# Second attention stage: logits as three products of high and low parts, and transposes three places behind the logits

## The reference, cut to what matters

```python
def diff_mixer(h, rel_bias, w_in, ..., lambda_init):
    proj = h @ w_in
    q = proj[..., :B_WIDTH].reshape(bsz, L, 2 * B_HEADS, B_HEAD_DIM) * (B_HEAD_DIM ** -0.5)
    k = proj[..., B_WIDTH:2 * B_WIDTH].reshape(bsz, L, 2 * B_HEADS, B_HEAD_DIM)
    v = proj[..., 2 * B_WIDTH:3 * B_WIDTH].reshape(bsz, L, B_HEADS, 2 * B_HEAD_DIM)
    ...
    def block(args):
        logits = jnp.einsum('bqmd,blmd->bmql', qb, k).astype(jnp.float32)
        logits = logits + jnp.moveaxis(bias, -1, 0)[None]
        logits = jnp.where((rel >= 0)[None, None], logits, -jnp.inf)
        p = jax.nn.softmax(logits, axis=-1).reshape(bsz, B_HEADS, 2, BLOCK_Q, L)
        a = p[:, :, 0] - lam * p[:, :, 1]
        return jnp.einsum('bhql,blhe->bqhe', a.astype(v.dtype), v)
```

## Time and profile before

| | us |
|---|---|
| median of 3 runs | 4052.26 |
| lowest and highest | 4047.88, 4061.18 |
| the profiled execution | 4043.49 |
| its span, first to last instruction | 4041.6 |
| TensorE busy | 3491.7 (86% of the span) |
| VectorE busy | 2131.5 (53%) |
| ScalarE busy | 2029.4 (50%) |
| GpSimd busy | 503.2 (12%) |
| mean granted TensorE clock | 0.935 |

### The profile page before, as it was taken

The page is one execution under the profiler, slowest core; times in us unless marked ns, Lnnn a source line. Parts: engine busy times, 40 slices in busy tenths (PEclk is TensorE's granted clock), DMA queues, the critical chain, the costliest instruction groups (busy, mean ns, idle before and its releaser), DMA issues. The chain is left out here.

```text
span 4041.6 us, 63580 instructions
## 1 busy us (share of the span) xinstructions
PE 3491.7 (86%) x18242; PEld 2545.4 (63%) x18242; DVE 2131.5 (53%) x5809; ACT 2029.4 (50%) x3495; POOL 503.2 (12%) x544
## 2 busy tenths in 40 slices
PE   7837798866799999998793999999978888889599
PEld 6725554446566666665683888889945555555487
DVE  2617989998455555554664000000067777777344
ACT  2516778972677777776224111111156666666222
POOL 1000045300111111111120111111000000000011
PEclk9968999986899999999896999999989999999789
DMA  6474277754232222222542222212121111110443
...
DMA packets 400008, 406.94 MB, mean 101 GB/s; under 512 B 73264, under 2 KB 325584, under 8 KB 398288
## 3 DMA queue, kind: packets, MB, share of 16 engines
...
## 5 line engine op out<-in xcount | busy, mean ns | idle before, releaser
L1119 DVE CUSTOM_DVE_ANT_0 a_att_sb_lg<-a_att_ps_s,mask 128x512 f32<-128x512 f32 (+3 forms) x512 | 302.2, 595 | 241.6 <-PE a_att_ps_s L1013 199.4
L393 ACT ACTIVATE b_qkgv_sb_o_lo<-b_qkgv_ps_acc 128x512 f32<-128x512 f32 x128 | 76.6, 599 | 637.5 <-PE b_qkgv_ps_acc L376 472.3
L1150 DVE MEMSET b_att_sb_mx<- 128x256 f32 x1 | 0.3, 272 | 721.6 <-PEq L88 721.6
L1193 ACT ACTIVATE a_att_sb_pT<-a_att_ps_t 128x512 f32<-128x512 f32 (+3 forms) x640 | 316.6, 530 | 106.7 <-PE a_att_ps_t L1029 98.4
L1185 ACT ACTIVATE b_att_sb_lg<-b_att_sb_lg,b_att_sb_negm 128x384 f32<-128x384 f32 (+15 forms) x256 | 305.7, 1198 | 112.5 <-DVE b_att_sb_negm L1127 112.0
L1121 DVE TENSOR_SCALAR_CACHE_REDUCE b_att_sb_lg<-b_att_ps_s 128x512 f32<-128x512 f32 (+3 forms) x512 | 289.8, 591 | 133.7 <-PE b_att_ps_s L1018 125.8
L1185 ACT ACTIVATE a_att_sb_lg<-a_att_sb_lg,a_att_sb_negm 128x384 f32<-128x384 f32 (+15 forms) x256 | 307.3, 1201 | 79.2 <-DVE a_att_sb_negm L1127 79.2
L1012 PE MATMUL a_att_ps_s<-a_att_sb_k,a_att_sb_q 128*128 128x512 f32 (+3 forms) x640 | 287.9, 450 | 67.0 <-DMA a_att_sb_k<-scratch_kT 45.2
L1029 PE MATMUL a_att_ps_t<-ident,a_att_sb_lg 128*128 128x128 f32 x2176 | 340.0, 279 | 0.0
L1018 PE MATMUL b_att_ps_s<-b_att_sb_k,b_att_sb_q 64*128 64x512 f32 (+3 forms) x1280 | 323.6, 592 | 14.5 <-DMA b_att_sb_k<-scratch_kT 9.9
L1540 DVE TENSOR_SCALAR_CACHE_REDUCE mask<-scores,threshold_bits 128x384 bf16<-128x384 f32 (+8 forms) x288 | 322.5, 1186 | 1.2
...
## 6 DMA issues: line engine op xcount, KB each, us to landing
...
a_att_sb_q<-scratch_qT SPq DMA_DIRECT2D x128, 128.0 KB
a_att_sb_q<-scratch_qT SPq DMA_DIRECT2D x256, 64.0 KB
...
```

What stands on the lines that cost most here:

```text
L1119: x = nc.vector.tensor_tensor_reduce(out, src, tab, 1.0, 2 * NEG, ALU.add, ALU.max, top[:, col:col + 1])
L1193: nc.scalar.activation(pT[:, r % 2, a:z, c:c + P], t_ps[:, n % TR, 0:z - a], ACT.Copy).then_inc(t_left, 1)
```

## The change

In `stage_attention` for M = 2, queries and keys come as high and low parts, each of the type F32R: `q` has a part index with two entries and so has `k`. A set of logits is three products for each map: high by high, low by high, high by low (query part first), accumulated in the same bank, map 0 and map 1 by turns. `LAG` is 3 for M = 2 and stays 2 for M = 1; `TAIL` follows from it. Each load of q or k is two transfers. In `b_qkgv` the jobs for q and k are of the kind "split", so both parts are written to memory.

```diff
--- before.py
+++ after.py
@@ -794,7 +794,6 @@
 OR = 2
 QS, OS, KPIECES = 4, 4, 4
 LR, LR2 = 4, 2
-LAG = 2
 PAIR = 2 * P
 
 PAIRS = [1, 3, 5, 7, 6, 4, 2, 0]
@@ -823,6 +822,7 @@
 
 
     V2 = M == 1
+    LAG = 2 if V2 else 3
     width = HD if V2 else P
     SR, TR = (2, 4) if V2 else (4, 2)
     NCHUNK = M * BEFORE[NB]
@@ -838,8 +838,8 @@
     NM = 4
 
     with Stage(nc, sems, name) as st:
-        q = st.sb("q", [P, QS, 2, PAIR], F32R) if V2 else st.sb("q", [P, QS, PAIR], F32)
-        k = st.sb("k", [P, 2, T], F32R if V2 else F32)
+        q = st.sb("q", [P, QS, 2, PAIR], F32R)
+        k = st.sb("k", [P, 2, T] if V2 else [P, 2, 2, T], F32R)
         v = st.sb("v", [P, 2, NB, width], F32)
         v_zero = st.sb("v_zero", [P, HD], F32) if V2 else None
         near, near_next = (st.sb(n, [P, M, NEAR], F32) for n in ("near", "near_next"))
@@ -900,15 +900,18 @@
                     for part in range(2):
                         sp.dma_start(q[(1 - part) * HD:(2 - part) * HD, r % QS, 1].bitcast(F32), q_dram[part, rows, cols]).then_inc(q_in[r % QS], 16)
                 else:
-                    sp.dma_start(q[:, r % QS], q_dram[0, ds(h * P, P), cols]).then_inc(q_in[r % QS], 16)
+                    for part in range(2):
+                        sp.dma_start(q[:, r % QS, part].bitcast(F32), q_dram[part, ds(h * P, P), cols]).then_inc(q_in[r % QS], 16)
 
             def load_k(h, piece):
                 keys = slice(piece * (T // KPIECES), (piece + 1) * (T // KPIECES))
-                dst = k[:, ds(h % 2, 1), keys].rearrange("p o t -> p (o t)")
                 if V2:
+                    dst = k[:, ds(h % 2, 1), keys].rearrange("p o t -> p (o t)")
                     sp.dma_start(dst.bitcast(F32), k_dram[0:2, ds(h * HD, HD), keys]).then_inc(k_in, 16)
                 else:
-                    sp.dma_start(dst, k_dram[0, ds(h * P, P), keys]).then_inc(k_in, 16)
+                    for part in range(2):
+                        dst = k[:, ds(h % 2, 1), part, keys].rearrange("p o t -> p (o t)")
+                        sp.dma_start(dst.bitcast(F32), k_dram[part, ds(h * P, P), keys]).then_inc(k_in, 16)
 
             def load_near(h):
 
@@ -1003,7 +1006,7 @@
                 b, (a, z) = ORDER[p], chunks(ORDER[p])[i]
                 cols = slice((b % 2) * P, (b % 2 + 1) * P)
                 if i == 0 and p % 2 == 0:
-                    loads = 48 if V2 else 16
+                    loads = 48 if V2 else 32
                     pe.wait_ge(q_in[p // 2 % QS], h * (NPAIR // QS * loads) + (p // 2 // QS + 1) * loads)
                 n = chunk_no(p, i, 0)
                 pe.wait_ge(s_left, h * NCHUNK + n + M)
@@ -1012,11 +1015,14 @@
                     nc.tensor.matmul(out, q[:, p // 2 % QS, 0, cols], k[:, slot, a:z], start=True, stop=False)
                     nc.tensor.matmul(out, q[:, p // 2 % QS, 1, cols], k[:, slot, a:z], start=False, stop=True).then_inc(s_done, 1)
                 else:
-                    for m in range(M):
-
-                        rows = slice(m * HD, (m + 1) * HD)
-                        nc.tensor.matmul(s_ps[:, (n + m) % SR, 0:z - a], q[rows, p // 2 % QS, cols], k[rows, slot, a:z],
-                                         start=True, stop=True).then_inc(s_done, 1)
+                    for j, (x, y) in enumerate(((0, 0), (1, 0), (0, 1))):
+                        for m in range(M):
+
+                            rows = slice(m * HD, (m + 1) * HD)
+                            mm = nc.tensor.matmul(s_ps[:, (n + m) % SR, 0:z - a], q[rows, p // 2 % QS, x, cols], k[rows, slot, y, a:z],
+                                                  start=(j == 0), stop=(j == 2))
+                            if j == 2:
+                                mm.then_inc(s_done, 1)
 
             def turn(h, p, i):
                 n, (a, z) = BEFORE[p] + i, quads(ORDER[p])[i]
@@ -1051,7 +1057,7 @@
 
             def place(h, p, before, par):
                 if h is not None and p == 0:
-                    pe.wait_ge(k_in, (h + 1) * (16 * KPIECES))
+                    pe.wait_ge(k_in, (h + 1) * (16 * KPIECES if V2 else 32 * KPIECES))
                     logits(h, 0, 0, par)
                 back, t = (h, p - LAG) if p >= LAG else (before, NB + p - LAG)
                 for i in range(4):
@@ -2087,8 +2093,8 @@
             hT = [sb(c, f"b_{n}", [P, KD, T], F32R) for n in ("hT_hi", "hT_lo")]
             stage_input(nc, sems, "b_in", x1, ada, 1, ident, hT)
             win = ins["b_w_in"][0].rearrange("(k p) n -> p k n", p=P)
-            stage_project(nc, sems, "b_qkgv", [Job("whole", hT, KD, lambda n: win[:, :, ds(n * P, P)], KD, HD ** -0.5, qT[0]),
-                                               Job("whole", hT, KD, lambda n: win[:, :, ds(n * P + D, P)], KD, 1.0, kT[0]),
+            stage_project(nc, sems, "b_qkgv", [Job("split", hT, KD, lambda n: win[:, :, ds(n * P, P)], KD, HD ** -0.5, qT[0], qT[1]),
+                                               Job("split", hT, KD, lambda n: win[:, :, ds(n * P + D, P)], KD, 1.0, kT[0], kT[1]),
                                                Job("silu", hT, KD, lambda n: win[:, :, ds(n * P + 3 * D, P)], KD, 1.0, gateT),
                                                Job("values", hT, KD, lambda n: win[:, :, ds(n * P + 2 * D, P)], KD, 1.0, v)])
         stage_attention(nc, sems, "b_att", 8, 2, ident, bias_dram, qT, kT, v, oT, sums, neglam=neglam)
```

## The result

| | before | after |
|---|---|---|
| median of 5 runs, us | 4052.26 | 4031.13 |
| lowest and highest | 4047.88, 4061.18 | 4027.53, 4037.09 |
| ratio after / before, 95% interval | | 0.995 [0.9936, 0.9965] |
| span of the profiled execution | 4041.6 | 4029.2 |
| mean granted TensorE clock | 0.935 | 0.925 |

The changed kernel is faster by 21 us (0.5%), and 50.5 were forecast. The sign was right and the time lies in the range, but more than half of the gain is missing. From here on a head is a head of the second attention stage and a place is one of its 16. Lines of the changed kernel are shifted: L1022 makes logits (L1018 before), L1035 the transposes (L1029), L1055 the products with the values (L1049), L1127 and L1125 are VectorE's evictions (L1121 and L1119), L1133 the negative maximum (L1127 before), L1145 the mix (L1139), L1184 the bias copy (L1178).

What follows compares the result with a forecast made beforehand. TensorE was taken as the bound, with a loop through VectorE on top. Heads -57, start +3.5 and end +3 gave -50.5 us: 3993 us for the profiled execution, 4001 from the median, range 3966 to 4045.

Steps and rivals of the forecast that it cites:

- the larger sums: Second attention stage: the longer of TensorE's and VectorE's time in each of 16 places, added up: 90.4 us a head.
- 90.4 + 4.2 - 2: Second attention stage: larger sums, plus other gaps kept from before, less TensorE's two-set lead at place 9: about 92.5 us.
- Each 512 set in 0.89 us: TensorE's logits: three one-pass products on each half, halves side by side, 0.89 us a set in place of 1.06.
- Rival (a): TensorE's logits: halves don't overlap in the one-pass type; 106.1 us a head, 4111 us in all, slower; chance 0.10.
- The wait for the mix goes, and waits for evictions come: Second stage: TensorE's transposes stop waiting for VectorE's mix (9.9 us a head); its logit products wait for VectorE's evictions instead.
- Split of the gain: Second stage: of 7.1 us a head less, some 5 from the three places and 2 from the three products.
- Rival (d): Second stage: products give nothing, only the places do; 94.6 us a head, 4018 us; chance 0.58 together with the forecast.
- The start, 3.5 us: Second stage's start: doubled q and k loads delay TensorE's first product by 3.5 us, bounds 2.3 and 6.5.
- The end, 3 us: Second stage's end: one more place of transposes and values with nothing beside it costs 3 us, bounds 0 and 6.
- Projections, nothing: Projections ahead of the stage: 64 extra VectorE evictions and second stores cost nothing, hidden behind a fully busy TensorE.
- (b), the clock: Second stage: TensorE's waits lower its clock; with two such stretches a head 99.3 us, total 4056 us; chance 0.14.
- (c), looser coupling: Second stage: engines couple more loosely and leftover gaps go too; 88.4 us a head, 3969 us; chance 0.13.

Runs made afterwards that it cites:

- the places alone: Kernel before with three places between logits and transposes, two products a set and single loads kept; edge at 6: 4024.1 us, edge at 11: 4004.3 us.

## Why the prediction was right and wrong

- **The step that failed** is the one from the larger sums to 92.5 us a head: "90.4 + 4.2 - 2". The 4.2 us of other gaps were carried over from the kernel before as they stood. Among them lay the loop's back edge, some 1 us a head there (place 5 at a full clock, 7.9 and 6.8 us with and without it), and the change moved it from place 5 to place 6 through `TAIL = LAG + 3`. The forecast moved transposes and values by one place and doubled the loads, and it left out the edge and what SP has in flight at it. The runs put the price at 36.4 us (35 by the ratios): the changed kernel against the same with its edge at 11. In the profiles some 32 us of it lie in place 6, and 5 in place 7, where the clock was lower in more heads. The trace of before had the row: VectorE's 1.84 us of "issue" with one instruction transfer beside it.
- **The base under the 4.2 us**: they were what 99.6 leaves over 85.5, TensorE's column alone, and 9.9 of waits, but were added to the sum of the larger columns, 90.4. For the kernel before those two bases differ by 4.9 us. That 92.6 came out within half a microsecond with the edge at 11 is in part luck; no run takes the 4.2 or the 2 us apart.
- **Each 512 set in 0.89 us**: right to the hundredth. Six passes of 0.226 us one after another would be 1.36, so the halves run side by side in the one-pass type too. Rival (a), halves one after another, is dead.
- **The wait for the mix goes, and waits for evictions come**: right, row for row.
- **92.5 us a head**: 97.0 in the changed kernel, 92.1 to 92.5 with the edge at 11. The total was right, although single places, as VectorE's maxima bound them, were not: place 0 takes 6.2 us where the table has 4.1, place 10 takes 5.7 where it has 7.7.
- **Split of the gain**: places 5 us a head and products 2. With the edge at 11, heads take 100.6 us before, 94.2 with the places and 92.1 with both. Products at distance three are worth 2.1 us a head in the traces, one profile of each; less the 5.5 us at the start, that would be 11 us in all. By the times (0.9886 and 0.9864, 9 us, with overlapping intervals) they can't be told from nothing. Rival (d) gave 94.6 us a head for the places alone, and 94.2 was measured. In the changed kernel, with its edge at 6, the products' part could not be seen at all.
- **The start, 3.5 us**: 5.5 (15.4 less 9.9), inside the bounds of 2.3 and 6.5.
- **The end, 3 us**: from the last L1133 to the stage's last output ScalarE took 7.7 us before and takes 10.8 now, 3.1 us more. **Projections, nothing**: TensorE's wait for its first keys begins at 2933.06 in both.
- **The sum against the profile**: 36 us in the heads and 2 at the start are the 38 us by which the profiled execution (4031.1 us in all) lies over the 3993 forecast for it. By medians the miss is 30 us, because the profiled execution of before lay 9 us under its median, and that of after lies on it.
- **(b), the clock**: it fell to 0.94 from 3000 to 3650 us, where the kernel before has 0.98, and in 20 us around TensorE's long wait to 0.74 (below). With the edge at 11 it is 0.97, so most of the fall goes with the stalls, which the rival didn't name. The rest is nearer to what it said, less work on TensorE: with the places alone and the edge at 11 the same stretch has 1.00, and with the products added 0.97. In the changed kernel it took 1.1 to 2.5 us in each place 7 that it reached, so it was a small part of the miss and not only a sign of it. How much of the products' gain it takes back isn't shown. **(c), looser coupling**: 88.4 us a head was not seen in any kernel.

```profile
3155.00:3175.00 20.00, 11.59 (x59) 7.02 (x57) 12.86 (x45) 8.56 (x13) 0.00 (x0) 0.74 0.21 58
```
